# Whole-array products with block-diagonal operands in the forward substitution of a hybrid RWKV-7, SSD and short-convolution layer

## The reference

```python
def step(s, inp):
    r_t, w_t, k_t, v_t, kh_t, b_t = inp
    sa = jnp.einsum('bhvk,bhk->bhv', s, kh_t)
    s = s * w_t[:, :, None, :] - sa[..., None] * b_t[:, :, None, :] + v_t[..., None] * k_t[:, :, None, :]
    return s, jnp.einsum('bhvk,bhk->bhv', s, r_t)
```

## Time and profile before

| | |
|---|---|
| runs | 1192.96, 1193.4, 1193.5 us |
| median | 1193.4 us |
| profiled execution | 1193.14 us |
| its span, first to last instruction | 1191.6 us |
| granted TensorE clock, mean | 0.997 of 2.4 GHz |
| TensorE busy | 1169.7 us, 98% |
| VectorE busy | 796.3 us, 67% |
| ScalarE busy | 573.9 us, 48% |
| GpSimd busy | 75.1 us, 6% |
| HBM | 164 GB/s over the span |

### The profile page before, as it was taken

The page is one execution under the profiler, slowest core; times in us unless marked ns, Lnnn a source line. Parts: engine busy times, 40 slices in busy tenths (PEclk is TensorE's granted clock), DMA queues, the critical chain, the costliest instruction groups (busy, mean ns, idle before and its releaser), DMA issues.

```text
span 1191.6 us, 23628 instructions
## 1 busy us (share of the span) xinstructions
PE 1169.7 (98%) x8534; PEld 1041.5 (87%) x8534; DVE 796.3 (67%) x1167; ACT 573.9 (48%) x828; POOL 75.1 (6%) x94
## 2 busy tenths in 40 slices
PE   6999999999999999999999999999999999999996
PEld 5999999899899998999989978888888888888885
DVE  4778768688686885868868764755545555556553
ACT  5556455354463644536546444544444444435442
POOL 2001011020110200102001011000000000000000
PEclk9999999999999999999999999999999999999998
DMA  6766545555455554553645545565666666658662
GB/s 169 208 166 169 159 120 145 147 139 160 119 152 135 142 160 118 158 154 106 165 136 155 149 138 181 157 216 171 212 201 192 189 197 194 192 180 288 193 196 95
DMA packets 254747, 197.24 MB, mean 166 GB/s; under 512 B 23943, under 2 KB 207472, under 8 KB 254064
## 3 DMA queue, kind: packets, MB, share of 16 engines
q1 hardware_dynamic: 252084, 195.56, 56.6%
q10 hardware_dynamic: 2620, 1.10, 0.4%
HBM read 193.71 MB, written 2.11 MB: 164 GB/s over the span
## 4 chain that ended last, share of the span: by engine, by line
PE 98%; DMA 1%; DVE 0%; ACT 0%; DVEq 0%; issue 0%; SPq 0%; ACTq 0%
PE ps L1167 16%; PE ps L1168 14%; PE ps L1169 14%; PE ps L1246 11%; PE ps L1248 11%; PE ps L1247 11%; PE ps L1493 2%; PE ps L1492 2%; PE ps L1491 2%; PE ps L1392 1%; PE ps L1278 1%; PE ps L1160 1%; PE ps L1359 1%; PE ps L1351 1%; PE ps L1372 1%; DMA o<-in_x 1%
## 5 line engine op out<-in xcount | busy, mean ns | idle before, releaser
L727 DVE TENSOR_TENSOR wlo<-raw,whi 128x1024 fp32r<-128x1024 f32 (+1 forms) x356 | 436.4, 1239 | 234.2 <-ACT whi L426 232.9
L426 ACT ACTIVATE whi<-raw 128x1024 fp32r<-128x1024 f32 (+1 forms) x356 | 372.9, 1054 | 308.8 <-PE ps L1248 178.9
L1167 PE MATMUL ps<-hhi,whi 128*128 128x256 f32 (+1 forms) x1440 | 417.9, 290 | 0.0
L1168 PE MATMUL ps<-hlo,whi 128*128 128x256 f32 (+1 forms) x1440 | 407.1, 283 | 0.0
L1169 PE MATMUL ps<-hhi,wlo 128*128 128x256 f32 (+1 forms) x1440 | 406.9, 283 | 0.0
L1167 PEld LDWEIGHTS ps<-hhi,whi 128*128 128x128 f32 (+1 forms) x1440 | 273.9, 190 | 13.4 <-issue 11.3
L1168 PEld LDWEIGHTS ps<-hlo,whi 128*128 128x128 f32 (+1 forms) x1440 | 274.2, 190 | 0.5
L1169 PEld LDWEIGHTS ps<-hhi,wlo 128*128 128x128 f32 (+1 forms) x1440 | 274.1, 190 | 0.3
L1246 PE MATMUL ps<-whi,hhi 128*128 128x512 f32 x384 | 151.0, 393 | 0.0
L1248 PE MATMUL ps<-whi,hlo 128*128 128x512 f32 x384 | 149.6, 389 | 0.0
L1247 PE MATMUL ps<-wlo,hhi 128*128 128x512 f32 x384 | 149.5, 389 | 0.0
(11 more groups left out here) (273 smaller groups left out, 1142.1 us busy)
## 6 DMA issues: line engine op xcount, KB each, us to landing
raw<-in_w_in SPq DMA_DIRECT2D x548, 256.0 KB, 3.1
raw<-in_w_branch SPq DMA_DIRECT2D x96, 256.0 KB, 3.7
raw<-in_w_out SPq DMA_DIRECT2D x64, 256.0 KB, 3.6
o<-in_x SPq DMA_DIRECT2D x4, 1024.0 KB, 6.9
acb<-acs_rows SPq DMA_DIRECT2D x7, 256.0 KB, 4.0
out_y<-lots SPq DMA_DIRECT2D x3, 512.0 KB, 4.6
lots<-in_final_norm_w SPq DMA_DIRECT2D x1, 1024.0 KB, 10.3
lots<-ad SPq DMA_DIRECT2D x32, 8.0 KB
```

Of the source, the lines that this page charges most:

```text
L426: sc.activation(whi[:, slot, :, 0:width], raw[:, slot, :, 0:width], ACT.Copy).then_inc(hi_done, 1)
L727: tt(wlo[:, slot, :, 0:width], raw[:, slot, :, 0:width], whi[:, slot, :, 0:width].bitcast(F32), ALU.subtract).then_inc(lo_done, 1)
L1167: mm(dst, a, khi, start=first, stop=False)
L1168: mm(dst, a, klo, start=False, stop=False)
```

## The change

Three things are changed.

First, `t32` becomes [128, 4, 128] and block-diagonal: a quarter has its four 32 x 32 blocks on the diagonal and zeros elsewhere. VectorE writes them in four additions of 32 rows. `uu` gets a buffer of its own; only the rows 0 to 31 of each chunk of 64 are written, the others stay zero. In `yy` only the rows 32 to 63 of each chunk are written. Each of these two copies becomes two instructions of 32 rows. GpSimd clears t32, uu and yy once, ahead of kdbd.

Second, with these operands every step is four whole-array products of 128 columns: one for each q in t = 20, 21 and 22, in place of 16, 8 and 8 tile products.

Third, the output visit is ordered anew: bon_ok is awaited first, then come the four products of uw and s4, the four of uw and kdbd, and only then the tile products with vt; yz_mm is released after the four tile products into A as before, which now stand behind the kdbd products.

```diff
-        uu = flat(9, 2)
...
-        t32p = sb("t32p", [P, 5, 32])
-        t32 = t32p[:, 1:5, :]
+        t32 = sb("t32", [P, 4, P])
+        uu = sb("uu", [P, 512])
...
             pool.wait_ge(s["sc_mm"], NG)
+            for t in (t32[:], uu[:], yy):
+                gp.memset(t, 0.0)
             gp.memset(kdbd, 0.0).then_inc(s["kdbd_z"], 1)
...
                     if t == V_P1 + 3:
                         act.wait_ge(s["u_mm"], j + 1)
-                        sc.activation(uu, B, ACT.Copy).then_inc(s["u_ok"], 1)
+                        for c in range(CPB):
+                            r = slice(64 * c, 64 * c + 32)
+                            op = sc.activation(uu[r, :], B[r, :], ACT.Copy)
+                        op.then_inc(s["u_ok"], 1)
                     if t == V_P1 + 4:
                         act.wait_ge(s["yx_mm"], j + 1)
-                        sc.activation(yy, A, ACT.Copy).then_inc(s["yx_ok"], 1)
+                        for c in range(CPB):
+                            w = slice(64 * c + 32, 64 * c + 64)
+                            op = sc.activation(yy[w, :], A[w, :], ACT.Copy)
+                        op.then_inc(s["yx_ok"], 1)
...
                         dve.wait_ge(s["d_mm"], j + 1)
-                        tt(t32, A[:, 0:P].rearrange("p (q n) -> p q n", q=4), tx[:, :, 0, :], ALU.add).then_inc(s["t32_ok"], 1)
+                        dve.wait_ge(s["kdbd_z"], 1)
+                        for i in range(4):
+                            r = slice(32 * i, 32 * i + 32)
+                            op = tt(t32[r, :, r], A[r, 0:P].rearrange("p (q n) -> p q n", q=4), tx[r, :, 0, :], ALU.add)
+                        op.then_inc(s["t32_ok"], 1)
...
                         for q in range(4):
-                            for i in (0, 2, 3, 1):
-                                r, n = slice(32 * i, 32 * i + 32), slice(q * P, q * P + P)
-                                if q == i == 0:
-                                    mm(B[0:64, n], t32[r, 0:2, :].rearrange("p q n -> p (q n)"), xx[r, n],
-                                       start=True, stop=True, skip_group_check=True)
-                                else:
-                                    op = mm(B[r, n], t32[r, q, :], xx[r, n], start=q == 0, stop=True, skip_group_check=True)
+                            n = slice(q * P, q * P + P)
+                            op = mm(B[:, n], t32[:, q, :], xx[:, n], start=q == 0, stop=True, skip_group_check=True)
...
                         for q in range(4):
-                            for c in range(CPB):
-                                r, w, n = slice(64 * c, 64 * c + 32), slice(64 * c, 64 * c + 64), slice(q * P, q * P + P)
-                                op = mm(A[w, n], s4[r, q, 2 * P + 64 * c:2 * P + 64 * c + 64], uu[r, n],
-                                        start=True, stop=True)
+                            n = slice(q * P, q * P + P)
+                            op = mm(A[:, n], s4[:, q, 2 * P:3 * P], uu[:, n], start=True, stop=True)
...
                         for q in range(4):
-                            for c in range(CPB):
-                                w, n = slice(64 * c + 32, 64 * c + 64), slice(q * P, q * P + P)
-                                if q == c == 0:
-                                    mm(B[0:64, n], t32p[w, 0:2, :].rearrange("p a n -> p (a n)"), yy[w, n], start=False,
-                                       stop=True, skip_group_check=True)
-                                else:
-                                    op = mm(B[w, n], t32[w, q, :], yy[w, n], start=False, stop=True, skip_group_check=True)
+                            n = slice(q * P, q * P + P)
+                            op = mm(B[:, n], t32[:, q, :], yy[:, n], start=False, stop=True, skip_group_check=True)
...
                         pe.wait_ge(s["uw_ok"], j + 1)
+                        pe.wait_ge(s["bon_ok"], j + 1)
                         for q in range(4):
                             r = slice(q * P, q * P + P)
                             mm(A[:, r], uw[:, q, :], s4[:, q, 3 * P:4 * P], start=q == 0, stop=False,
                                skip_group_check=True)
                         for q in range(4):
                             b, e = q // 2, q % 2
+                            mm(ps[:, 6 + b, e * P:e * P + P], uw[:, q, :], kdbd[:, b, 1, :, 64 * e:64 * e + 64],
+                               start=e == 0, stop=False, skip_group_check=True)
+                        for q in range(4):
+                            b, e = q // 2, q % 2
                             r, h, i = slice(q * P, q * P + P), slice(64 * e, 64 * e + 64), slice(64 - 64 * e, 128 - 64 * e)
                             op = mm(A[i, r], vt[:, b, h], s4[:, q, P:2 * P], start=False, stop=q >= 2, skip_group_check=True)
                         op.then_inc(s["yz_mm"], 1)
-
-                        pe.wait_ge(s["bon_ok"], j + 1)
                         for b in range(2):
-                            for e in range(2):
-                                h = slice(64 * e, 64 * e + 64)
-                                mm(ps[:, 6 + b, e * P:e * P + P], uw[:, 2 * b + e, :], kdbd[:, b, 1, :, h],
-                                   start=e == 0, stop=False, skip_group_check=True)
```

More of the change, by code:

```diff
@@ L328, in _ @@
                          (ones[:], 1.0), (causal[:], 0.25), (restart[:], 1.0), (st[:], 0.0), (sol_t, 0.0),
-                         (lorat[:], 0.0), (pq[:], 0.0), (xp[:], 0.0), (scx[:], 0.0), (t32p[:], 0.0), (eps3[:, 0:1], 1e-6),
+                         (lorat[:], 0.0), (pq[:], 0.0), (xp[:], 0.0), (scx[:], 0.0), (eps3[:, 0:1], 1e-6),
                          (eps3[:, 1:2], 64e-5)):
```

## The result

The changed kernel takes 1195.19 us (median of 19 runs, 1194.47 to 1195.81) against 1193.16 of before (19 runs, 1192.68 to 1193.71). The ratio is 1.0016 with a 95% interval of 1.0009 to 1.0023: 2.0 us slower, less than the 0.2% that the prediction counted as a measurable change. Of the 18.8 us that the prediction counts as saved in TensorE's own work, nothing shows in the time. The question for the experiments is therefore whether the work was saved at all, and what gave it back.

The account below looks back on a forecast made before the run. TensorE, busy for 98% of the span, was taken as the bound. Per iteration - 0.73 (three visits less stalls) + 0.89 (output visit) = + 0.16, eight times + 1.3 on 1193.4: 1194.7 us, range 1193 to 1197 (0.64).

Parts of the forecast that it names:

- The three visits on TensorE: Rewritten visits at t = 20, 21, 22: whole-array products save 0.66, 0.33 and 0.65, together 1.64 us an iteration.
- t32 in four additions: VectorE's four 32-row additions run one after the other, 1.17 us; no stall at t = 20, or up to 0.1.
- The copy of u: ScalarE's paired copy, queued behind a tanh delayed by the token shift, stalls TensorE 0.78 us, between 0.13 and 0.95.
- The release: Time from a producer's end to the start of the waiting matmul, allowed at 0.15 us as an upper bound.
- The copy of yy: ScalarE's paired copy into yy ends late for its product: stall 0.13 us, between 0 and 0.3.
- The chain behind yz_mm: Output visit: yz_mm fires 0.89 us later, no slack up to L1418, so it costs 0.89 (0.79 to 0.94), not saving 0.71.
- the hold rule: VectorE instruction whose operands start in another 32-partition quadrant waits for the previous one; additions take 1.17 us, not 0.92.
- The sum: Whole loop: - 0.73 + 0.89 = + 0.16 us an iteration, eight times + 1.3 us, giving 1194.7 us.
- B: Rival: vector and scalar pieces overlap, net - 0.20 to - 0.40 us an iteration, 1191.8 to 1190.2 us; chance 0.13.
- C: Rival: only TensorE's own time counts, 18.8 us saved, 1174.6 us; chance 0.05.
- D: Rival: restart after each pause (u, yy, t = 24) costs 0.20 us, 1199.5 us; half price 1197.1; chance 0.14.
- E: Rival: pauses lower TensorE's clock to the 1.2 GHz level for part of each iteration, 2.3 us more, 1213 us; chance 0.04.

Follow-up runs that it names:

- the last kernel above: Changed kernel with shift, quadrant order, masked copies, t = 24 work and L984/L990 moved, plus state product awaiting the copy of yz, not z_in: 1174.85 us, ratio 0.9844.

## Why the prediction was right

- **The three visits on TensorE,** minus 1.64 us an iteration: right. The group of four takes 0.89 and its dense successors come without the 0.20 of a mode switch; the last kernel above, with nothing waiting, wins the whole sum.
- **t32 in four additions,** 1.17 us: measured 1.19, and the split behind it at 1.22. The product at t = 20 starts when due (142.33 + 0.12 = 142.45), no stall, as said. The tanh L556 starts 143.93 - 136.95 = 6.98 us behind the visit at t = 18, against 143.30 - 137.34 = 5.96 before: a microsecond later, as said.
- **The copy of u,** a stall of 0.78: 0.72, and 0.11 for the restart that I had not added (1.16 in place of 1.05), 0.83 in all. The release was overrated, 0.15 against 0.05 (the copies end at 144.26 + 1.17 = 145.43, the matmul starts at 145.48), and the restart left out; that the two errors nearly cancel is luck. The cause, the tanh behind the shift, is shown by the kernel that moves the shift.
- **The copy of yy,** 0.13: the number is right by luck. It was forecast as a wait for the copies, with a release of 0.15; with the release of 0.05 that wait is only some 0.02 us. What costs the 0.13 is the longer first record, 0.11, for which the prediction adds nothing.
- **The chain behind yz_mm,** + 0.89: measured + 0.93. The mechanism is shown by the kernel with the visit alone, which is slower by 0.80 a round (6.26 against 5.46, within the bounds of 0.79 to 0.94). Two terms were mis-sized and nearly cancel, again by luck: the release from L990 to L1416 is 0.06 (156.68 to 156.74), not 0.15, so this chain had 0.09 of slack before, where the prediction says it had none; and L984 is held for 0.12. 0.89 - 0.09 + 0.12 = 0.92. I had read the hold rule only for the instructions next to the additions and missed its reach to the next reader of PSUM.
- **The sum,** + 0.16 an iteration, 1.3 us: + 0.25 by the loop's period, 2.0 us. The predicted 1194.7 is 0.5 us below the measured 1195.19. So close a hit owes something to errors that cancel; what the experiments bear out is the mechanism, two covered chains that come to bind.
- **Rivals.** B is out: no overlap, neither in the four additions nor in the pairs of copies. C is what the change is worth when nothing waits, 1174.6, and the last kernel measured 1174.85; in the changed kernel itself it is out. D: a restart costs 0.11 us where a group of whole products follows a pause, not 0.20, and it was at u and yy only. E is out: the granted clock stays at 1.00, the 2.4 GHz level, in the iteration with all three pauses, and the page's mean is 0.997 as before:

```profile
136.90:213.80 76.90, 74.86 (x689) 71.02 (x689) 60.00 (x106) 40.08 (x67) 7.35 (x6) 1.00 0.53 143
```

## What to carry to other kernels

On an engine that is busy for 98% with work of several streams, count for each producer that is moved later not only what it saves there but how long the chain behind its semaphore is, and compare that with the work left to cover it: here four matmuls of 0.89 us in all, ahead of one increment, cost 0.80 us a round, and the 0.71 that the new order saves did not show until the chain was freed. Work that is queued in the same engine ahead of a critical copy, and could run in that engine's idle time before it, is the first thing to move; it wins nothing while the chain is covered and 10 us when it is not. And when one instruction is split by partition ranges, count the pieces in full: here they did not overlap (four additions of 0.29 took 1.19 us), and the last of them delayed a reader of PSUM 13 us behind.

## What the runs showed of the hardware

- 16 diagonal 32 x 32 fp32 tiles (one of them widened to 64 columns of the array) with 128 columns each cost 1.55 us inside a full-array stream (1.35 and a switch of 0.20 out), where four zero-padded whole-array products cost 0.89.
- On VectorE, the last reader of PSUM still counted 13 us and a dozen instructions later: the full-height L984 followed the split after 1.26 us when that reader began at row 96, and after 1.14 when it began at row 0.
- Instructions on other partition ranges than the one before ran one after the other on both engines: four additions 1.19, pairs of ScalarE copies 1.17 to 1.19, where a full-height neighbour starts 0.08 to 0.11 before the end of the one ahead.
- Restarting whole-array fp32 products after a pause lengthened their first record by 0.11 us, even where the pause itself was under 0.02 (the group at yy).
- Pauses of 0.7 and 1.3 us in an iteration of 77 us, among dense matmuls, left the granted clock at 1.00, the 2.4 GHz level.
